# Value projections with x as the stationary operand, later waits in the attention stages, and a recurrent output computed tile by tile on ACT and POOL

## What is computed

```
h = x @ w_in                       # fq fk fv | sq sk sv | dq dk dv | iq ik iw | gates
o_fox = softmax(q k' / 8 + c_q - c_k, causal) v      # 6 heads, c = cumsum(log f)
o_sb  = stick_breaking(q, k) v                       # 5 heads
score = sum_h iw_h * relu(iq_h ik')                  # index; top 128 keys per query
o_dsa = softmax(q k' / 8 on the chosen keys) v       # 5 heads, one key head
merged = sum_b sigmoid(g_b) * (o_b @ w_up_b)
x = layer_norm(a x + merged @ w_out)
x = layer_norm(a x + relu(x @ w_ff_in)**2 @ w_ff_out + sigmoid(x @ w_ple_gate) * (p @ w_ple))
```

```
u = rms_norm(x) @ w_in
a, b = gates(conv4(u_lru));  h_t = a_t h_(t-1) + b_t      # a scan over tokens
y = [nsa(q, k, v) * silu(z_n),  h * silu(z_l),  conv(...) @ w_pw2 * silu(z_c)]
x = x + y @ w_out
```

## Time and profile before

| | |
|---|---|
| median of 3 runs | 2674.05 us (2673.57 to 2676.76) |
| the profiled execution's own time | 2674.82 us |
| its span, first to last instruction | 2673.0 us |
| TensorE busy / matmuls | 2579.5 us (97%) / 12484 |
| VectorE, ACT, POOL busy | 58%, 43%, 40% |
| mean granted TensorE clock | 0.991 |
| traffic | 224 MB, 84 GB/s |

### The profile page before, as it was taken

One profiled execution on the slowest core, in us unless ns is written; L12 is line 12 of the kernel. 1 busy time (PEld: TensorE's weight loads), 2 busy tenths in 40 slices (PEclk: granted clock), 3 DMA queues, 4 the chain that ended last, 5 costly groups with the idle time before them and its releaser, 6 DMA issues.

```text
span 2673.0 us, 35546 instructions
## 1 busy us (share of the span) xinstructions
PE 2579.5 (97%) x12484; PEld 1992.9 (75%) x12484; DVE 1544.0 (58%) x2510; ACT 1145.3 (43%) x1984; POOL 1065.7 (40%) x430
## 2 busy tenths in 40 slices
PE   8999999999999899999999999997999999999998
PEld 6867666788888688676677888885887776887776
DVE  6138747853223670576488334227688766787765
ACT  3344544433222343454535233235337554347554
POOL 4432223344445344222133544442446612447612
PEclk9999999999999999999999999999999999999999
DMA  5221112222223242111122322221223211223211
GB/s 200 94 83 48 56 46 78 82 95 94 94 94 104 77 124 92 66 57 47 48 93 81 109 96 94 94 100 58 88 93 126 72 41 48 94 95 125 73 41 56
DMA packets 64203, 224.27 MB, mean 84 GB/s; under 512 B 7888, under 2 KB 8016, under 8 KB 64080
## 3 DMA queue, kind: packets, MB, share of 16 engines
q1 hardware_dynamic: 63504, 221.06, 24.2%
q10 hardware_dynamic: 576, 1.57, 0.2%
HBM read 216.57 MB, written 2.10 MB: 82 GB/s over the span
## 4 chain that ended last, share of the span: by engine, by line
PE 82%; DVE 7%; DVEq 4%; ACT 3%; issue 2%; POOL 1%; ACTq 0%; DMA 0%; SPq 0%
PE bank L396 23%; PE bank L398 22%; PE bank L397 22%; PE bank L545 3%; PE bank L572 3%; DVEq L2241 2%; PE bank L558 2%; POOL w_lo L454 1%; PE bank L548 1%; PE bank L820 1%; PE bank L1169 1%; PE bank L794 1%; DVE ffn_sum L1691 1%; PE bank L803 1%; PE bank L1220 0%
## 5 line engine op out<-in xcount | busy, mean ns | idle before, releaser
L454 POOL TENSOR_TENSOR w_lo<-w_raw,w_hi 128x1024 fp32r<-128x1024 f32 x404 | 1014.7, 2519 | 1582.7 <-ACT w_hi L405 1576.7
L396 PE MATMUL bank<-x_hi,w_hi 128*128 128x512 f32 x2112 | 856.7, 406 | 29.8 <-DVE x_lo L2470 10.6
L398 PE MATMUL bank<-x_hi,w_lo 128*128 128x512 f32 x2112 | 829.4, 393 | 0.0
L397 PE MATMUL bank<-x_lo,w_hi 128*128 128x512 f32 x2112 | 828.4, 392 | 0.0
L405 ACT ACTIVATE w_hi<-w_raw 128x1024 fp32r<-128x1024 f32 x400 | 419.5, 1055 | 416.3 <-PE bank L398 355.3
L396 PEld LDWEIGHTS bank<-x_hi,w_hi 128*128 128x128 f32 x2112 | 399.8, 189 | 133.7 <-issue 32.6
L398 PEld LDWEIGHTS bank<-x_hi,w_lo 128*128 128x128 f32 x2112 | 399.7, 189 | 86.2
L397 PEld LDWEIGHTS bank<-x_lo,w_hi 128*128 128x128 f32 x2112 | 400.4, 190 | 78.3 <-issue 2.9
L396 PE MATMUL bank<-rhs_hi,w_hi 128*128 128x512 f32 x624 | 246.5, 395 | 6.1 <-DVE rhs_lo L1593 6.1
L397 PE MATMUL bank<-rhs_lo,w_hi 128*128 128x512 f32 x624 | 244.5, 392 | 0.0
L398 PE MATMUL bank<-rhs_hi,w_lo 128*128 128x512 f32 x624 | 244.2, 391 | 0.0
(11 more groups left out here) (409 smaller groups left out, 3203.2 us busy)
## 6 DMA issues: line engine op xcount, KB each, us to landing
w_raw<-w SPq DMA_DIRECT2D x404, 512.0 KB, 3.4
work<-proj SPq DMA_DIRECT2D x60, 64.0 KB, 2.0
ln_in<-x SPq DMA_DIRECT2D x4, 512.0 KB, 7.3
out<-residual SPq DMA_DIRECT2D x8, 256.0 KB, 2.1
p_raw<-p ACTq DMA_DIRECT2D x2, 512.0 KB, 3.5
constants<-con SPq DMA_DIRECT2D x1, 455.0 KB, 10.3
cos<-cos SPq DMA_DIRECT2D x1, 256.0 KB, 10.4
sin<-sin SPq DMA_DIRECT2D x1, 256.0 KB, 10.3
```

The lines of the kernel that those rows point to most:

```text
L396: nc.tensor.matmul(out, wh, xh, start=first, stop=False)
L397: nc.tensor.matmul(out, wh, xl, start=False, stop=False)
L398: S.last = nc.tensor.matmul(out, wl, xh, start=False, stop=last)
L454: S.nc.gpsimd.tensor_tensor(S.wl[s][:, :], S.raw[s][:, :], S.wh[s][:, :].bitcast(F32), ALU.subtract).then_inc(S.lo_ready[s], 1)
```

## The change

1. The first kind's units 8 to 11 become one group whose 512 output columns are three fox value tiles and the first stick tile, computed token-major: for each of 8 k-tiles and 4 token blocks, x is the stationary operand and the weights are moved, into four banks at once (`values`). ACT copies the banks straight to `vt`. The host packs these four weight units anew. Tile 25 moves from unit 8 to unit 12; ACT's `dup` copies move from unit 8 to 12.
2. Only tiles 4, 5 and 16 are still turned, after units 16 and 23; the wait for the turned tiles moves from before index step 0 to before index step 2.
3. In `pairs_pe`, pair 0 does fill, scores 1, fill, turn 0 (was: scores 1, fill, turn 0, fill). This holds for fox, DSA and NSA.
4. The last DSA gate unit is spread over 6 calls instead of 8, and ACT takes a finished gate unit before the next exponentials instead of after the copy.
5. Second kind: the wait for the copies of the turned compressed probabilities moves to turn 0 of NSA. POOL first splits unit 48, then makes `la` tile by tile (four times 128 x 512); ACT rounds each tile to x_hi; POOL subtracts tile by tile. The wait for unit 45 on POOL falls away, and `out_fill` waits for all four tiles and two of the convolution branch's products.

```
-A_ORDER = (16, 17, 18, 20, 21, 22, 23, 24, 25, 0, 1, 2, 3, 4, 5, 6, 7, 8, 9, 10, 11, 12, 13, 14, 15)
+A_ORDER = (16, 17, 18, 20, 21, 22, 23, 24, 0, 1, 2, 3, 25, 4, 5, 6, 7, 8, 9, 10, 11, 12, 13, 14, 15)
+A_VALUES = 8
+A_TURNED = (4, 5, 6)
-VT_AT = {11: (0, 1), 13: (2, 3), 15: (4, 5), 23: (6,)}
+VT_AT = {16: (0, 1), 23: (2,)}
...
     (sp_stream)
+        ahead = {A_ORDER.index(tile) + ROT_LAG: n for n, (tile, _, _) in enumerate(ROPE)}
...
     (pool_program)
-        x4h, x4l = S.xh[:, 0:4 * SEQ], S.xl[:, 0:4 * SEQ]
+        pool_split(S, pool, 0, GB(L, B_OUTL))
         pool.wait_ge(S.lru_scanned, L + 1)
-        pool.wait_ge(S.unit_done[B_LAST % SLOTS], GB(L, B_LAST) + 1)
-        nc.gpsimd.tensor_tensor(x4h, S.lrt[:, :], S.zl[:, :], ALU.mult)
-        nc.gpsimd.tensor_tensor(S.la[:, :], S.lrt[:, :], S.zl[:, :], ALU.mult)
-        pool.drain()
-        nc.gpsimd.tensor_tensor(x4l, S.la[:, :], x4h.bitcast(F32), ALU.subtract).then_inc(S.lru_done, 1)
-        splits(1, GB(L, B_OUTL))
+        for t in range(4):
+            nc.gpsimd.tensor_tensor(seq(S.la, t), seq(S.lrt, t), seq(S.zl, t), ALU.mult).then_inc(S.lru_y, 1)
+        for t in range(4):
+            pool.wait_ge(S.lru_hi, L * 4 + t + 1)
+            nc.gpsimd.tensor_tensor(seq(S.xl, t), seq(S.la, t), seq(S.xh, t).bitcast(F32), ALU.subtract).then_inc(S.lru_done, 1)
+        for s in range(1, SLOTS):
+            pool_split(S, pool, s, GB(L, B_OUTL))
...
     (pairs_pe)
+        if n == 0:
+            fill(n, 0)
+            scores(n + 1)
+            fill(n, 1)
+            turn(n)
+            continue
...
+DSA_CALLS = (8, 8, 6)
...
     (a_tensor)
+        def values():
+            g = G(A_VALUES)
+            for k in range(KT):
+                s, c = divmod(k, 2)
+                if c == 0:
+                    pe.wait_ge(S.lo_ready[s], g + 1)
+                wh, wl = (w[s][:, c * SEQ:(c + 1) * SEQ] for w in (S.wh, S.wl))
+                for t in range(QB):
+                    if k == 0:
+                        pe.wait_ge(S.bank_free[t], g + 1)
+                    xh, xl = (x[:, k * SEQ + t * P:k * SEQ + (t + 1) * P] for x in (S.xh, S.xl))
+                    nc.tensor.matmul(S.ps[t][:, :], xh, wh, start=(k == 0), stop=False)
+                    nc.tensor.matmul(S.ps[t][:, :], xh, wl, start=False, stop=False)
+                    m = nc.tensor.matmul(S.ps[t][:, :], xl, wh, start=False, stop=(k == KT - 1))
+                    if k == KT - 1 and t < QB - 1:
+                        m.then_inc(S.v_summed, 1)
+                if c:
+                    m.then_inc(S.unit_done[s], 1)
...
-        pe.wait_ge(S.vt_done, (L + 1) * A_NVT)
         pe.wait_ge(S.rope_done, (L + 1) * len(ROPE))
         pe.wait_ge(S.dup_ready, (L + 1) * 2)
         for n, (b, h) in enumerate(idx_steps()):
             if n >= 4:
                 pe.wait_ge(S.relu_done, L * 24 + n - 3)
+            if n == 2:
+                pe.wait_ge(S.vt_done, (L + 1) * len(A_TURNED))
...
-                 lambda n, x: gate_share(S, pe, L, DSA_FILL[n // QB], 2 * (n % QB) + x, 8), dsa_ready, lead=last_of_stick)()
+                 lambda n, x: gate_share(S, pe, L, DSA_FILL[n // QB], 2 * (n % QB) + x, DSA_CALLS[n // QB]), dsa_ready, lead=last_of_stick)()
...
     (a_scalar)
+        def values():
+            def free(s):
+                act.wait_ge(S.unit_done[s], G(A_VALUES) + 1)
+                act_split(S, act, A_VALUES + s, G(A_VALUES))
+            for s in range(SLOTS - 1):
+                free(s)
+            for t in range(QB):
+                if t < QB - 1:
+                    act.wait_ge(S.v_summed, L * (QB - 1) + t + 1)
+                else:
+                    act.wait_ge(S.unit_done[SLOTS - 1], G(A_VALUES) + 1)
+                nc.scalar.activation(vt[:, t, 0:SEQ], S.ps[t][:, :], ACT.Copy).then_inc(S.bank_free[t], 1)
+            free(SLOTS - 1)
...
-        pairs_act(S, act, S.dsa, L * 20, L * 12, dsa_pairs(S), lambda n: round_gates(DSA_FILL, n))
-        round_gates(DSA_FILL, 3 * QB)
+        pairs_act(S, act, S.dsa, L * 20, L * 12, dsa_pairs(S), lambda n: None,
+                  before=lambda n: round_gates(DSA_FILL, n, DSA_CALLS))
...
     (out_fill)
-            pe.wait_ge(S.lru_done, L + 1)
+            pe.wait_ge(S.lru_done, (L + 1) * 4)
+            pe.wait_ge(S.mc_y, L * 4 + 2)
...
     (b_tensor)
-        pe.wait_ge(S.cpt_copied, L * 2 + 2)
         def nsa_ready(n, what):
             if what == "turn" and n == 0:
-                return [(S.mc_y, L * 4 + 4)]
+                return [(S.mc_y, L * 4 + 4), (S.cpt_copied, L * 2 + 2)]
...
     (b_scalar)
         z(B_ZN, S.zn, 3)
+        for t in range(4):
+            act.wait_ge(S.lru_y, L * 4 + t + 1)
+            nc.scalar.activation(seq(S.xh, t), seq(S.la, t), ACT.Copy).then_inc(S.lru_hi, 1)
...
     (units_a)
+    wide = np.concatenate([m.reshape(P, KT, P) for m in proj[A_VALUES:A_VALUES + SLOTS]], axis=2)
+    proj[A_VALUES:A_VALUES + SLOTS] = [wide[:, 2 * s:2 * s + 2].reshape(P, KT * P) for s in range(SLOTS)]
```

More of the change, by code:

```diff
@@ L232, in plan @@
     S.vt_done = sem("vt_done")
+    S.v_summed = sem("v_summed")
     S.logf_in = sem("logf_in")
@@ L438, in sp_stream @@
     for L in range(DEPTH):
-        first, last = L * A_GROUPS + ROT_LAG // SLOTS, L * A_GROUPS + -(-(ROT_LAG + len(ROPE)) // SLOTS)
+        ahead = {A_ORDER.index(tile) + ROT_LAG: n for n, (tile, _, _) in enumerate(ROPE)}
+        first, last = L * A_GROUPS + min(ahead) // SLOTS, L * A_GROUPS + max(ahead) // SLOTS + 1
         loads(done, first)
@@ L442, in sp_stream @@
             for s in range(SLOTS):
-                n = (g - L * A_GROUPS) * SLOTS + s - ROT_LAG
-                if n < len(ROPE):
-                    sp_rot(S, sp, L, n)
+                u = (g - L * A_GROUPS) * SLOTS + s
+                if u in ahead:
+                    sp_rot(S, sp, L, ahead[u])
                 load(s, g, slice(g * SLOTS + s, g * SLOTS + s + 1))
@@ L1109, in gate_fill @@
             S.last.then_inc(S.unit_done[s], 1)
+DSA_CALLS = (8, 8, 6)
 def gate_share(S, pe, L, fill, c, calls):
+    if c >= calls:
+        return
     first, units = fill
@@ L1138, in turn_v @@
         def turn_v(v):
-            tile = A_VT[v]
+            tile = A_VT[A_TURNED[v]]
             taken(tile)
             if v >= 2:
-                pe.wait_ge(S.vt_done, L * A_NVT + v - 1)
+                pe.wait_ge(S.vt_done, L * len(A_TURNED) + v - 1)
             for t in range(QB):
@@ L1145, in turn_v @@
                                         S.qkv[:, tile * SEQ + t * P:tile * SEQ + (t + 1) * P], ident)
-                if v == A_NVT - 1 and t == 0:
+                if v == len(A_TURNED) - 1 and t == 0:
                     m.then_inc(S.unit_done[A_SPARE % SLOTS], 1)
@@ L1152, in a_tensor @@
         pe_side_by_side(S, pe, range(wide), G(0), S.xh, S.xl, S.x_ready, L * 2 * KT)
+        def values():
[16 more added lines that the diff above has]
+                    m.then_inc(S.unit_done[s], 1)
         for u in range(wide, len(A_ORDER)):
+            if A_VALUES <= u < A_VALUES + SLOTS:
+                if u == A_VALUES:
+                    values()
+                continue
             pe_unit(S, pe, u, G(u), S.ps[u % SLOTS][:, :], S.xh, S.xl).then_inc(S.unit_done[u % SLOTS], 1)
@@ L1336, in a_scalar, with round_gates @@
         gate_takes(IDX_FILL, 12, 11)
-        def round_gates(fill, n):
+        def round_gates(fill, n, calls=(8, 8, 8)):
             if n == 0:
@@ L1342, in round_gates @@
             for x in range(2):
-                gate_takes(fill[i], 2 * QB, 2 * m + x)
+                gate_takes(fill[i], calls[i], 2 * m + x)
         def fox_after(n):
@@ L2406, in mix_lo @@
             if k == 0:
-                dve.wait_ge(S.lru_done, L + 1)
+                dve.wait_ge(S.lru_done, (L + 1) * 4)
             dve.wait_ge(S.mn_hi, L * 4 + k + 1)
```

10 lines of the change are left out of this document (6 added, 4 removed).

## The result

The changed kernel takes 2660.16 us (median of 4 runs, 2659.11 to 2662.23) beside 2675.41 us of the kernel before (4 runs, 2673.57 to 2678.71): ratio 0.9944, 95% interval 0.9932 to 0.9957. Forecast: 2660.0. The profiled execution took 2659.11 us around a span of 2657.3 us, 15.7 less than the span before.

What follows compares the result with a forecast made beforehand. TensorE, busy 97% of the span, was taken as the bound. Terms -3.5 -4.0 -1.7 +0 -2.7 -1.7 -0.7 = -14.3 took 2674.8 to 2660.5, less 0.8 to the median: 2660 us, range 2652 to 2668.

Steps and rivals of the forecast that it cites:

- (d): Merge after DSA: six shares and earlier eviction of the last gate unit gain 0.8 us per layer, 1.7 in all.
- (e): Recurrent branch, last attention's start: POOL's early split delays VectorE's scans, leaving 0.6 us gained in layer 1, 0.1 in layer 2.
- (a): Value group in the projections: two double turns fewer in each of two layers save 3.5 us; stationary x costs nothing.
- Rival 4: Value group: stationary x loads no longer hidden, up to 0.19 us per matmul, +36 us, 2696; chance 0.04.
- (b): Index stage: moving the wait for turned value tiles before step 2 saves 2.0 us per layer, 4.0 in all.
- The clock's -1.7: Layer 2's index stage: low clock, 6 us at 0.72, counted as gone with the gap ahead of it, 1.7 us.
- (c): Pair 0 with fill before the second scores: fox 0 us, DSA 1.4 us per layer gained, 2.7 in all.
- rival 2: Waits only change place in fox, DSA and the merge: some 5 us off in all, 2669.5; chance 0.09.
- the low clock behind it I leave in: Behind the merge's gap: the low clock was expected to stay, still two us of gaps, so no gain was counted.
- rival 3: Merge: full clock comes back, 3.4 to 6.8 us more gained, in the middle 5, so 2655; chance 0.12.
- the one from there to scores 1: Last attention, layer 1: after the second pointwise unit's 2.2 us wait, fill at 2113.3, scores 1 at 2115.4 behind ACT's table load.
- Rival 1: Recurrent branch: POOL's split doesn't hold VectorE's scans, so 4.2 us more is gained, 2656; chance 0.15.

Runs made afterwards that it cites:

- experiment 1: The changed kernel with POOL's split of the first pointwise unit's slot moved behind its four products: 2653.03 us, ratio 0.9921 to the kernel before.

## Why the prediction was right, and where it was not

The time was right to a tenth of a us, which is luck in good part: (d) came out 2.8 us better than forecast and (e) 2.3 worse, and they nearly cancelled.

- **(a) Value units, -3.5.** Held: 1.8 us per layer, steps of 0.23 us. Rival 4 (stationary x loads) is refuted.
- **(b) Index stage, -4.0.** Held: 2.0 us per layer were gained up to fox, and putting the wait back costs 4.0 between the traces. **The clock's -1.7** had the right size in this pair of traces (1.5) but a wrong reason. With the gap of 2.12 us kept, the stretch was low in 1 index stage of 6 (the kernel before, the value group alone, the index wait put back, two layers each). It was not "gone with the gap".
- **(c) Fox 0, DSA -2.7.** Held: 0.1 and -2.8. The waits forecast for fox (1.2 us before scores 2 and a new one before scores 3) are there. The reason given for 0 was half wrong: scores 3 follow turn 0, and not a chain that can't be shortened. So rival 2 (the waits only change place) holds for fox alone; the gains of the index stage, DSA and the merge stayed to the end of their layers.
- **(d) Merge, -1.7.** The term was too small in two ways. The wait fell to 1.51 (1.7 forecast), and 1.2 us per layer were gained instead of 0.8. And "the low clock behind it I leave in" failed in layer 1: 2.2 us came back there. This is a part of rival 3, which I had at 0.12 with 3.4 to 6.8 us. Layer 2 kept a stretch of 0.79, as before, so the rest of its price did not come. Over all traced kernels: the 12 us behind the wait held a low stretch in 6 merges of 6 where it was 3.03 us long, and in 2 of 20 where it was 1.5 us (layer 2 of the changed kernel and of the one with fox's old order).
- **(e) Recurrent branch, -0.7.** The mechanism held in each link: the scans are held by 2.2 us, the wait for silu_z_nsa is 2.27 us (2.2 forecast). The step that failed is the one from there to scores 1, which left out that a new wait of this length can bring a low clock with it. Scores 1 came 1.5 us later than the working had them, and the unit behind the wait ran low for 3 us. In layer 1 the low stretch at 2115 us went in exchange (clock 1.00 from 2114 to 2122), but in layer 2 two new ones came. So the term was -0.9 in layer 1 and +2.5 in layer 2: +1.6 instead of -0.7. Rival 1 is refuted by experiment 1. Its price (4.2) was right for the waits (4.5), and short of the 7 that the median shows.
- **The clock outside the change** gave 1.6 and took 1.6, and the start of layer 1 gave 0.6. I had it nowhere; it is why single terms can't be read from medians here.

The Trainium skill ("SBUF — State Buffer", Who interferes with whom) says that whichever starts first holds the shared pair for its whole instruction. The trace agrees so far as the 2.15 us that the scans lost are nearly the length of one split (2.36 at the merge). That a running queue of scans would keep the pair is refuted: POOL's split got in among the four.

## What to carry to other kernels

An operation of POOL that loses its wait will run earlier, perhaps among VectorE's operations on SBUF: look up who is waiting behind those before you call it free. It may be one line's place that decides whether a whole rewrite pays (here one split gave back 4.5 of the 5.6 us that the new branch was worth). Where TensorE's waits are short and many, weigh each by what the clock does behind it, too: at the merge a wait of 3 us brought a low stretch every time, one of 1.5 us seldom. When you fill a gap on TensorE, put what other engines wait for (the turn) ahead of the filler.

## What was not expected of the hardware

- **Clock and length of the wait.** At the merge, 3.03 us: low in 6 of 6; 1.5 us: low in 2 of 20; in the index stage 2.12 us: low in 1 of 6. Whether a stretch is low can change with a shift of a few us far ahead: the value group alone lost the stretch at its index stage without touching the wait.
- **A row of scans isn't safe.** The scans took 2.15 us longer because of one split of POOL, which was itself held for 0.3 us (2.69 where the one at the merge has 2.36).
